# Ten gate panels in the seven-product form, with keys and values kept in DRAM meanwhile

## The reference

```python
h = rmsnorm(x, g_mix); proj = h @ w_in
za, zb, zc, zg = split(proj)                       # 1024, 1536, 512 and 3072 columns
ya = chunked_spatial_gating(gelu(za)) @ w_branch_a
yb = short_gated_conv(zb) @ w_branch_b
yc = multiscale_pool(zc) @ w_branch_c
gates = sigmoid(zg.reshape(1, S, 3, D) + b_gate)
x = x + (gates[0] * ya + gates[1] * yb + gates[2] * yc) @ w_o
x = x + cross_attention(x, mem)                    # 4 heads, keys and values from mem
x = x + (silu(h2 @ w_gate) * (h2 @ w_up)) @ w_out  # hidden width 2816
return rmsnorm(x, g_final)
```

## Time and profile before

| | us |
|---|---|
| median of three runs | 911.29 (911.28 to 911.63) |
| the profiled execution, its own time | 911.21 |
| its span in the trace | 909.5 |
| TensorE busy (matmuls) | 898.2, 99% of the span |
| VectorE busy | 517.4, 57% |
| ScalarE busy | 349.9, 38% |
| GpSimd busy | 55.8, 6% |

### The profile page before, as it was taken

The page is one execution under the profiler, slowest core; times in us unless marked ns, Lnnn a source line. Parts: engine busy times, 40 slices in busy tenths (PEclk is TensorE's granted clock), DMA queues, the critical chain, the costliest instruction groups (busy, mean ns, idle before and its releaser), DMA issues.

```text
span 909.5 us, 12096 instructions
## 1 busy us (share of the span) xinstructions
PE 898.2 (99%) x4880; PEld 782.0 (86%) x4880; DVE 517.4 (57%) x607; ACT 349.9 (38%) x479; POOL 55.8 (6%) x59
## 2 busy tenths in 40 slices
PE   9999999999999999999999999999999999999997
PEld 8898888888888888888888888889999999888886
DVE  4685346682234245365455465998888887433333
ACT  5655322342222323233234242555455545322223
POOL 0101000000000000015200054000000000000000
PEclk9999999999999999999999999999999999999999
DMA  8942221322222222222221122222233223322212
GB/s 341 350 181 93 93 104 76 110 93 93 93 92 93 92 92 92 92 93 96 90 93 47 47 93 93 93 93 92 92 120 110 92 92 127 128 93 93 93 47 92
DMA packets 15184, 97.52 MB, mean 107 GB/s; under 512 B 1712, under 2 KB 1840, under 8 KB 4272
## 3 DMA queue, kind: packets, MB, share of 16 engines
q1 hardware_dynamic: 13536, 93.33, 28.0%
q10 hardware_dynamic: 1152, 2.17, 0.7%
q0 software_dynamic: 464, 1.57, 0.6%
HBM read 94.97 MB, written 2.10 MB: 107 GB/s over the span
## 4 chain that ended last, share of the span: by engine, by line
PE 90%; DVE 4%; ACT 2%; DMA 2%; issue 1%; SPq 0%; POOLq 0%; POOL 0%; ACTq 0%; DVEq 0%
PE psum L1261 30%; PE psum L1263 30%; PE psum L1262 29%; DMA xt<-xt 2%; DVE wl L763 1%; DVE tl L763 1%; ACT wh L371 1%; PE psum L1487 0%; ACT pr L577 0%; PE psum L1313 0%; PE psum L1614 0%; ACT xt L418 0%; SPq L281 0%; DVE w7l L763 0%; DVE sm L1031 0%
## 5 line engine op out<-in xcount | busy, mean ns | idle before, releaser
L763 DVE TENSOR_TENSOR wl<-raw,wh 128x2048 fp32r<-128x2048 f32 (+1 forms) x56 | 116.8, 2094 | 150.1 <-ACT wh L371 150.0
L1261 PE MATMUL psum<-hh,wh 128*128 128x512 f32 x384 | 149.7, 390 | 0.0
L1263 PE MATMUL psum<-hh,wl 128*128 128x512 f32 x384 | 149.4, 389 | 0.0
L1262 PE MATMUL psum<-hl,wh 128*128 128x512 f32 x384 | 149.4, 389 | 0.0
L1261 PE MATMUL psum<-th,w7h 128*128 128x256 f32 x504 | 142.7, 283 | 1.2 <-ACT snap L371 1.2
L1262 PE MATMUL psum<-tl,w7h 128*128 128x256 f32 x504 | 142.6, 283 | 0.0
L1263 PE MATMUL psum<-th,w7l 128*128 128x256 f32 x504 | 142.6, 283 | 0.0
L371 ACT ACTIVATE wh<-raw 128x2048 fp32r<-128x2048 f32 (+1 forms) x56 | 96.1, 1726 | 62.2 <-PE psum L1263 62.2
L1261 PEld LDWEIGHTS psum<-th,w7h 128*128 128x128 f32 x504 | 96.7, 192 | 1.4 <-ACT snap L371 1.4
L1262 PEld LDWEIGHTS psum<-tl,w7h 128*128 128x128 f32 x504 | 96.8, 192 | 0.0
L1263 PEld LDWEIGHTS psum<-th,w7l 128*128 128x128 f32 x504 | 96.8, 192 | 0.0
(11 more groups left out here) (228 smaller groups left out, 1612.0 us busy)
## 6 DMA issues: line engine op xcount, KB each, us to landing
raw<-weights SPq DMA_DIRECT2D x79, 1024.0 KB, 4.8
vraw<-weights SPq DMA_DIRECT2D x2, 1024.0 KB, 15.7
xt<-xt SPq DMA_DIRECT2D x1, 2048.0 KB, 16.6
X<-x SPq DMA_DIRECT2D x2, 1024.0 KB, 27.5
vraw<-weights SPq DMA_DIRECT2D x3, 512.0 KB, 10.2
memt<-memt SPq DMA_DIRECT2D x1, 1024.0 KB, 22.6
out<-outb SPq DMA_DIRECT2D x4, 256.0 KB, 2.0
out<-outb ACTq DMA_DIRECT2D x4, 256.0 KB, 2.5
```

Of the source, the lines that this page charges most:

```text
L763: return V.tensor_tensor(dst, v, f32(hi), ALU.subtract)
L1261: nc.tensor.matmul(dst, lh, rh, start=start, stop=False, **kw)
L1262: nc.tensor.matmul(dst, lh, rl, start=False, stop=False, **kw)
L1263: return nc.tensor.matmul(dst, ll, rh, start=False, stop=stop, **kw)
```

## The change

**Gate stage.** The first two of the twelve gate panels stay as they were. For the other ten, TensorE does seven products (`gate_seven`), on token sums `gth` and `gtl` that are made once, and on weight sums made for each panel. VectorE makes the latter in place in `raw` (`gate_prep`, `gate_prep_lo`). ScalarE makes the high parts and the four copies s1, s5, u2 and u3 into `gsnap` (`keep`). VectorE adds these to the two tiles (`gate_add`), and the sigmoid reads them after that. In the code h counts the six pairs of gate panels, h = 0 being the old form; the first panel of a pair is called A below, the second B, and the branch panel behind them C.

**Room.** The token sums take the place of the keys and values (`kh`, `kl`, `vh`, `vl`), which are written to a DRAM tensor and read back after the last gate panel (eight transfers of 1 MB, issued by ScalarE). The weight sums take half of `X`, so the input is read a second time into `X` (2 MB).

**Token scaling.** The gain is now applied together with the row scale, in place in `X`, and the copies and subtractions read that.

**First transfers.** Three pieces instead of five for the first two value panels, two instead of three for memory. Value panel 3 is loaded and split ahead of the squares of `xt`, not behind them.

**Feed-forward.** In the first seven-product panel, ScalarE copies u2 ahead of the sums s13 (`first_window`). All semaphores for a panel's first tile are one, `first_tile`.

```diff
-V_PIECES = ((0, 1), (1, 2), (2, 4), (4, 6), (6, 8))
-MEM_PIECES = ((0, 2), (2, 4), (4, 8))
+V_PIECES = ((0, 2), (2, 4), (4, 8))
+MEM_PIECES = ((0, 4), (4, 8))
...
+            sp.dma_start(vraw[:, 3, :], weights[V0 + 3]).then_inc(v_panel[1], 16)
             sp.dma_start(xt[:], xt_in).then_inc(xt_here, 16)
-            sp.dma_start(vraw[:, 3, :], weights[V0 + 3]).then_inc(v_panel[1], 16)
...
+            act.wait_ge(kv_kept, 64)
+            quarter = lambda q: X[:, q // 2 * 4:q // 2 * 4 + 4, q % 2 * Q:(q % 2 + 1) * Q]
+            for i, q in enumerate((0, 1, 3, 2)):
+                act.wait_ge(sums_gate, i + 1)
+                copy(gth[:, i], quarter(q)).then_inc(gth_ready, 1)
...
+            for h in range(1, 6):
+                first, second = gate_panel_of(h, 0), gate_panel_of(h, 1)
+                gate_plain_hi(*first)
+                if h > 1:
+                    gate_sigmoid(h - 1, 1, 0)
+                gate_pair_hi(*first, 0)
+                if h > 1:
+                    gate_sigmoid(h - 1, 1, 1)
+                gate_pair_hi(*first, 1)
+
+                keep(first[1], 0, "s1")
+                gate_plain_hi(*second)
+                keep(first[1], 0, "s5")
+                keep(first[1], 0, "u2")
+                gate_pair_hi(*second, 0)
+                gate_pair_hi(*second, 1)
+                keep(first[1], 0, "u3")
+
+                keep(second[1], 1, "s1")
+                split_hi(second[0] + 1)
+                keep(second[1], 1, "s5")
+                keep(second[1], 1, "u2")
+                for t in range(2):
+                    gate_sigmoid(h, 0, t)
+                keep(second[1], 1, "u3")
...
             for n in range(2):
                 split_lo(XI0 + n + 1)
+                if n == 0:
+                    token_sum_lo()
...
+            def gate_prep(n, i):
+
+                w, blocks, p = raw_flat(n % SLOTS), raw_blocks(n % SLOTS), n % 2
+                dve.wait_ge(hi_a, i + 1)
+                lo(gate_lo[p][0], blocks[:, 1:4], gate_hi[p][0]).then_inc(lo_a, 1)
+                dve.wait_ge(lo_a, i + 1)
+                chain(V.tensor_tensor(w[:, 2], w[:, 2], w[:, 0], ALU.subtract))
+                chain(V.tensor_tensor(w[:, 0], w[:, 0], w[:, 1], ALU.subtract))
+                V.tensor_tensor(w[:, 1], w[:, 1], w[:, 2], ALU.add).then_inc(s2_ready, 1)
+                dve.wait_ge(s2_ready, i + 1)
+                V.tensor_tensor(w[:, 3], w[:, 3], w[:, 1], ALU.subtract).then_inc(s4_ready, 1)
...
+                gate_prep(n, i)
+                merge(h - 1, 0)
+                gate_prep_lo(n, i)
+                merge(h - 1, 1)
+
+                merge(h - 1, 2)
+                gate_prep(n + 1, i + 1)
+                merge(h - 1, 3)
+                gate_prep_lo(n + 1, i + 1)
+
+                gate_add(n, i, 0)
+                split_lo(n + 2)
...
+                pe.wait_ge(lo_a, i + 1)
+                pe.wait_ge(low_read, 4 * h + 2 * j + 2)
+                gate_product(right[:, Q:S], n, 0, 1, "B11", start=True).then_inc(p1_done, 1)
+                pe.wait_ge(lo_s13, i + 1)
+                gate_product(left[:, Q:S], n, 1, 0, "T1", start=True).then_inc(p5_done, 1)
+                pe.wait_ge(s1_kept, i + 1)
+                gate_product(right[:, Q:S], n, 1, 1, "T2").then_inc(p6_done, 1)
+                pe.wait_ge(s5_kept, i + 1)
+                gate_product(left[:, 0:Q], n, 0, 2, "B21")
+                pe.wait_ge(u2_kept, i + 1)
+                pe.wait_ge(lo_ready, n + 1)
+                gate_product(right[:, Q:S], n, 2, 0, "T3").then_inc(p7_done, 1)
+                gate_product(left[:, Q:S], n, 2, 1, "B22").then_inc(p3_done, 1)
+                pe.wait_ge(u3_kept, i + 1)
+                gate_product(right[:, 0:Q], n, 0, 0, "T4").then_inc(panel_done, 1)
```

More of the change, by code:

```diff
@@ L43 @@
 NF = 4
+NG = 10
 NS = HT - NF
@@ L414, in _ @@
                     v_panel_hi(i, half)
[L415 to L418, removed]
+            act.wait_ge(xt_here, 16)
+            for t in range(TT):
+                nc.scalar.activation(xt[:, t, :], xt[:, t, :], ACT.Square, accum_out=small(XS + t)).then_inc(sums_x, 1)
             split_hi_halves(K0)
@@ new lines, in keep @@
+            def keep(i, j, which):
+                left, right = bank[2 * j], bank[2 * j + 1]
+                done, kept, dst, src = {
+                    "s1": (p1_done, s1_kept, gsnap[:, 0, 0:Q], right[:, Q:S]),
+                    "s5": (p5_done, s5_kept, gsnap[:, 1, Q:S], left[:, Q:S]),
+                    "u2": (p6_done, u2_kept, gsnap[:, 0, Q:S], right[:, Q:S]),
+                    "u3": (p7_done, u3_kept, gsnap[:, 1, 0:Q], right[:, Q:S])}[which]
+                act.wait_ge(done, i + 1)
+                if i and which == "s1":
+                    act.wait_ge(gate_sum, i)
+                elif i and which == "s5":
+                    act.wait_ge(up_sum, i)
+                copy(dst, src).then_inc(kept, 1)
@@ L1004, in residual_lo @@
+            gate_add(GA0 + 16, NG - 1, 1)
+            split_lo(WO0)
+            for t in range(4):
+                merge(5, t)
+                if t:
+                    merged_lo(4 + t - 1)
+            merged_lo(7)
             def residual_lo(i, gain, first, high, low):
@@ L1392, in _ @@
             for n in range(2):
[L1393 removed]
+                fm_panel(XI0 + n, h_hi, h_lo, first_tile, [(gc_ready, 2 * n + t + 1) for t in range(2)])
             for g in range(4):
@@ new lines, in _, with gate_product @@
+            for q, name in enumerate(("T1", "T3", "T2", "T4")):
+                tokens[name] = lambda k, q=q: (gth[:, q, k, :], gtl[:, q, k, :])
+            def gate_product(dst, n, group, which, name, start=False):
+                hi, low = gate_hi[n % 2][group], gate_lo[n % 2][group]
+                for k in range(4):
+                    ins = mm3(dst, hi[:, which, k, :], low[:, which, k, :], *tokens[name](k),
+                              start and k == 0, k == 3, skip_group_check=True)
+                return ins
@@ L1664 @@
         for half in range(2):
-            ga += [gates[4 * b + 2 * half:4 * b + 2 * half + 2], branch[b][half:half + 1]]
+            for i in range(4 * b + 2 * half, 4 * b + 2 * half + 2):
+                first, second = gate_cols[:, 256 * i:256 * i + P], gate_cols[:, 256 * i + P:256 * (i + 1)]
+                ga.append(gates[i:i + 1] if b + half == 0 else gate_blocks_of(first, second)[None])
+            ga.append(branch[b][half:half + 1])
     w_k, w_v = np.split(a["w_xkv"][0], 2, axis=1)
```

319 lines of the change are left out of this document (202 added, 117 removed).

## The result

The changed kernel takes 913.56 us (median; 912.52 to 914.77), the kernel before 911.28 (911.01 to 911.78). The ratio is 1.0023, with a 95% interval of 1.0015 to 1.003: slower by 0.15 to 0.3%. The prediction was 910.1, in a range up to 912.8, so both its number and its sign are wrong. One of 14 executions of each kernel, at 1417.9 and at 988.5 us, was far slower and is counted in the two medians alone; without it the changed kernel's median is 913.0. The execution profiled is of the lower group: 912.73 us, with a span of 911.0.

A forecast was written before the change was run, and what follows sets the result against it. TensorE, busy 898.2 of 909.5 us, was taken as the bound. Terms -2.4 + 3.05 - 1.37 + 0.4 - 0.94 = -1.26 on a median of 911.29 gave 910.0, rounded to 910.1 us; range 906.5 to 912.8.

The forecast's parts named there:

- Slower, by the clock: Rival: the stall before PC0 drops TensorE's clock to 1.2 GHz, losing 2.5 us, for 912.5 us; 15%.
- The wait before PC0: TensorE stalls before PC0 because VectorE's weight split comes late, behind token-sum low parts and convolution; +3.05 us.
- the likeliest case: The main forecast for the whole kernel: 910.1 us, own range 908.3 to 911.9, given 62%.
- The first matmul's delay: At the start, the larger first memory piece delays the first matmul by 0 to 2.1 us; taken as +0.4.
- First transfers: At the start: -1.37 us from loading value panel 3 earlier, +0.4 from the larger first memory piece.
- Gate stage: Ten gate panels with seven products: a pair takes 32.16 instead of 32.64 us, five times; -2.4 us.
- the five stalls: In each pair's first gate panel TensorE waits 1.02 us for copy u3; 5.6 of 8.0 us go back.
- Feed-forward: In the first seven-product feed-forward panel, copy u2 is on time and 0.4 of stall stays; -0.94 us.
- Token sums: Making token sums delays VectorE's low part of PC0, so TensorE stalls there; +3.05 us, bounds 0 and 3.5.
- the stall of value panel 3: Near 27 us, TensorE's wait for value panel 3 goes because that panel is split first; -1.37 us.
- the larger transfers: Stores of keys and values, their read-back and the second read of `X` were costed at nothing.
- 8.0 us of removed work: Ten gate panels go from 10.88 to 10.08 us each: 8.0 us less if nothing stalls.

The follow-up runs named there:

- run 4: Kernel before, with VectorE repeating part of PC0's low part eight times so TensorE waits 3.0 us there: 916.21 us (1.0055).
- run 8: Kernel before, with seven extra low parts ahead of the second GC panel's low part, making TensorE wait 3.2 us there: 916.2 us (1.0049).
- run 9: Kernel before, with seven extra low parts ahead of PC0's low part, for a shorter TensorE wait: 913.16 us (1.002).
- run 2: Changed kernel with only the gate stage's copy u3 of panel A moved ahead of both pairs of panel B: 909.01 us (0.9976).
- run 6: Changed kernel with the token sums' low parts and copy u3 moved, plus 30 pairs of warming matmuls instead of 24: 903.68 us (0.9917).
- run 10: Changed kernel with 30 pairs of warming matmuls instead of 24 and nothing else: 912.48 us (1.0009).
- run 5: Changed kernel with the token sums' low parts and copy u3 moved, plus the old, smaller first pieces: 903.18 us (0.9917).
- run 3: Changed kernel with both the token sums' low parts moved behind the second PC panel's and copy u3 moved ahead of B's pairs: 905.24 us (0.9929).
- run 1: Changed kernel with the token sums' low parts moved behind the low part of the second PC panel: 908.06 us (0.997).
- run 7: Changed kernel with token sums' low parts and u3 moved, old first pieces, and VectorE's fourth branch tile behind A's first sum: 903.01 us (0.9903).

## Why the prediction was wrong

**The step that failed** is "*Slower, by the clock*", and the 15% it got. The wait before PC0 was placed and sized well (3.05, measured 3.21 against what TensorE was ahead), but the likeliest case charged it with itself alone. In the trace of before no stall was above 1.3 us, so its rows could not tell that a wait of 3 us costs more; I let their silence count as evidence. Runs 4 and 8 show in a trace each that such a wait brings the clock to 1.2 GHz, and by their times that it does so in most executions; run 9 shows that one of 1.7 doesn't. The price that the rival worked out, 2.5 us, was too high: 1.6 in the profiled execution. The warning of the Trainium skill on which the prediction drew (TensorE: Matmul & The Clock Gate, the section on why this matters), that an idle gap between bursts brings back the half rate, agrees with these runs, though not with every execution.

**A second fall was in no case.** The first matmul's delay was costed as a delay. It also makes the gap behind the warming matmuls longer, and in about half of the executions (six of 13 by the times) the clock falls there too, for another 1.5 us. Run 2's trace shows both falls in one execution, and run 6 takes the upper group away. This is why the median is not 912.6 but above it.

**How the two add up.** With 1.6 us for the first fall the forecast would have been 911.7. The terms below are 1.1 more in sum, which gives 912.8 for the lower group, measured as 912.5 to 913.0. The second fall adds 1.5 for the upper.

**Terms that were mis-sized,** and together put the kernel at 911.1 instead of 910.0 before any fall (four executions of run 10 had 911.0 to 911.2):
- First transfers: +0.96 instead of +0.4. The argument was that the number of packets sets the pace and stays the same for the first piece. ScalarE got its piece 0.96 later, and what is gained up to the value panels' end is 0.50 instead of 0.97. Run 5 confirms the size, 0.8 to 0.9.
- Gate stage: -2.01 instead of -2.4. Place, number and releaser of the five stalls were right; a pair took 32.24 instead of 32.16. The working says that without them 5.6 us come free, and the runs agree only in sum: 4.1 with u3 moved, 1.7 more with VectorE's tile moved. The prediction saw one wait and not the next one behind it, a sum of VectorE that is later from the third pair on.
- Feed-forward: -0.86 instead of -0.94. Token sums: +3.21 instead of +3.05.

**What held:** the five waits for `gsnap` of 0.9 us in the first panel of each pair and none in B, the wait before PC0 released by VectorE's weight split, the stall of value panel 3 gone, 0.3 left in the first feed-forward panel, and the larger transfers (stores, read-back, `X`) costing nothing that a wait shows. So of 8.0 us of removed work 2.0 arrived, and the waits before PC0 and at the start took more than that.

**What stays open.** Why a wait of some 3 us is followed by a fall in one execution and not in the next, and why the executions with one lie 1.4 to 2.8 us above those without in runs 4, 8 and 10. Also why, by the times, none of 13 executions of the changed kernel went without a fall before PC0, and 4 of 11 did with more warming matmuls. And the kernel before has no two groups in some 60 executions, with the same 48 warming matmuls. Either the clock doesn't fall at its start, or the fall is hidden there: TensorE waits for value panel 3 at 27 us in any case, and my estimate from those rows is that 27.80 - 26.53 = 1.27 of the 1.6 us would go into that wait. The change took this wait away, and with it what may have hidden the fall; no run tests it. For the same reason a fall at the start would add only some 0.3 in runs 4 and 8, which are built on the kernel before.

## What to carry to other kernels

Ask of each wait of TensorE that an edit adds not only how long it is, but whether it is longer than any that the trace shows with the clock at 1.00; above that, charge the half rate behind it as the likely case. Where a kernel's times fall in groups some 1.5 us apart, look at the clock in windows of a microsecond behind each gap, the first one above all. And when a copy that holds TensorE up is moved, follow the next one behind it through every repetition of the loop, since an operation that doubles in later ones can make it late again.

## What the runs showed of the hardware

- Behind waits of 3.0 and 3.2 us TensorE's clock stood at 1.2 GHz for some 3.4 us. This began between 0.4 us ahead of the first matmul behind the wait (run 4, where the clock was down from 152.6) and 1.4 us after it (the changed kernel), and by the times not in every execution; at the start of run 3 it was low with the first one. All eight falls in the kept traces, three of them at the start, lasted 3.4 us, by windows of one microsecond. Behind 1.7 it didn't fall. At the start, a gap of 2.09 us was followed by no fall (run 1) and one of 2.12 us by a fall (run 7).
- The same 48 warming matmuls took 7.04, 7.10, 7.86 and 8.44 us in four executions.
- The first 256 KB of memory landed 6.8 us after their issue; as one piece of 512 KB ScalarE had it 0.96 us later.
